# Differential attention: a wait per head for the rotated query, and one copy per unit for the turned probabilities, ahead of the next exponentials

## The reference, cut to what matters

```python
q = (h @ wq).reshape(B, L, N_HEADS, 2, HEAD_DIM)
q = partial_rope(q, pos) * (HEAD_DIM ** -0.5)
...
s = jnp.einsum('bqhcd,bkhcd->bhcqk', qblk, k).astype(jnp.float32)
...
p = jax.nn.softmax(s, axis=-1)
a = p[:, :, 0] - lam * p[:, :, 1]
return jnp.einsum('bhqk,bkhe->bqhe', a.astype(v.dtype), v)
```

## Time and profile before

| | us |
|---|---|
| median of 3 runs | 3104.79 |
| the three runs | 3104.3, 3104.79, 3112.43 |
| the profiled execution | 3102.6 |
| its span, first to last instruction | 3100.6 |

### The profile page before, as it was taken

One profiled execution on the slowest core, in us unless ns is written; L12 is line 12 of the kernel. 1 busy time (PEld: TensorE's weight loads), 2 busy tenths in 40 slices (PEclk: granted clock), 3 DMA queues, 4 the chain that ended last, 5 costly groups with the idle time before them and its releaser, 6 DMA issues.

```text
span 3100.6 us, 61224 instructions
## 1 busy us (share of the span) xinstructions
PE 2918.1 (94%) x21508; PEld 2783.9 (90%) x21508; DVE 2027.0 (65%) x4439; ACT 1544.0 (50%) x3349; POOL 583.7 (19%) x632
## 2 busy tenths in 40 slices
PE   8898889999999988889989999999989999999998
PEld 7688879999999987788889999999878799986998
DVE  6759877677677655578877666666573655555565
ACT  7442345555555544542445555555543455554554
POOL 4512670010010033015720000000130310012100
PEclk9899999999999988799999999999985999998899
DMA  4045317676676533145146555555441045541454
GB/s 154 16 130 164 113 58 224 210 232 223 210 230 205 183 117 109 55 141 166 61 146 209 184 183 183 183 183 183 156 129 55 1 135 185 169 130 34 143 183 136
DMA packets 140810, 458.19 MB, mean 148 GB/s; under 512 B 15792, under 2 KB 33584, under 8 KB 140656
## 3 DMA queue, kind: packets, MB, share of 16 engines
q1 hardware_dynamic: 135120, 436.75, 44.7%
q0 software_dynamic: 5536, 19.47, 2.2%
HBM read 446.65 MB, written 9.50 MB: 147 GB/s over the span
## 4 chain that ended last, share of the span: by engine, by line
PE 87%; DVE 5%; ACT 4%; POOL 2%; issue 1%; DMA 0%; DVEq 0%; POOLq 0%; ACTq 0%; SPq 0%
PE banks L784 64%; PE banks L941 7%; PE banks L964 3%; PE banks L1063 2%; PE banks L805 2%; POOL x_lo L2393 2%; PE banks L861 1%; PE banks L1149 1%; ACT w_hi L501 1%; PE banks L1179 1%; ACT arena L1389 1%; PE banks L1227 1%; PE banks L815 1%; ACT arena L1673 1%; DVE onehot L1987 1%
## 5 line engine op out<-in xcount | busy, mean ns | idle before, releaser
L508 DVE TENSOR_TENSOR w_lo<-ring,w_hi 128x512 fp32r<-128x512 f32 x1464 | 1019.5, 703 | 748.0 <-ACT w_hi L501 741.1
L501 ACT ACTIVATE w_hi<-ring 128x512 fp32r<-128x512 f32 x1464 | 916.7, 631 | 928.1 <-PE banks L784 885.7
L784 PE MATMUL banks<-x_hi,w_hi 128*128 128x256 f32 (+2 forms) x3136 | 911.2, 291 | 46.5 <-POOL x_lo L2393 21.3
L784 PE MATMUL banks<-x_lo,w_hi 128*128 128x256 f32 (+2 forms) x3136 | 902.0, 288 | 0.0
L784 PE MATMUL banks<-x_hi,w_lo 128*128 128x256 f32 (+2 forms) x3136 | 899.6, 287 | 0.0
L784 PE MATMUL banks<-gated_hi,w_hi 128*128 128x256 f32 x2560 | 727.3, 284 | 10.0 <-DVE gated_lo L2046 9.8
L784 PE MATMUL banks<-gated_hi,w_lo 128*128 128x256 f32 x2560 | 726.7, 284 | 0.0
L784 PE MATMUL banks<-gated_lo,w_hi 128*128 128x256 f32 x2560 | 725.5, 283 | 0.0
L784 PEld LDWEIGHTS banks<-x_hi,w_hi 128*128 128x128 f32 x3136 | 609.4, 194 | 57.6 <-issue 39.8
L784 PEld LDWEIGHTS banks<-x_lo,w_hi 128*128 128x128 f32 x3136 | 609.8, 194 | 0.6
L784 PEld LDWEIGHTS banks<-x_hi,w_lo 128*128 128x128 f32 x3136 | 610.3, 195 | 0.0
(11 more groups left out here) (325 smaller groups left out, 2941.5 us busy)
## 6 DMA issues: line engine op xcount, KB each, us to landing
ring<-in_peer_v SPq DMA_DIRECT2D x256, 512.0 KB, 3.6
ring<-in_peer_u SPq DMA_DIRECT2D x192, 512.0 KB, 3.5
arena<-in_peer_u SPq DMA_DIRECT2D x64, 512.0 KB, 3.6
ring<-in_mlp_up SPq DMA_DIRECT2D x64, 512.0 KB, 3.5
ring<-in_mlp_down SPq DMA_DIRECT2D x64, 512.0 KB, 3.5
ring<-w_peer_query SPq DMA_DIRECT2D x32, 512.0 KB, 3.5
ring<-w_fox_proj SPq DMA_DIRECT2D x24, 512.0 KB, 3.5
ring<-w_nsa_proj SPq DMA_DIRECT2D x20, 512.0 KB, 3.5
```

Of the source, the lines that this page charges most:

```text
L501: act.activation(w_hi[:, hn % SPLITS], raw_half(hn), ACT.Copy).then_inc(hi_ready, 1)
L508: dve.tensor_tensor(w_lo[:, hn % SPLITS], raw_half(hn), w_hi[:, hn % SPLITS].bitcast(F32), ALU.subtract)\
L784: mm = pe.matmul(out, w_at(w), x, start=start and j == 0, stop=stop and j == 2, skip_group_check=True)
```

## The change

Three edits, all in `attend_diff` of TensorE and ACT. The one wait for all eight heads becomes a wait per unit of the first query block for its own head. The 16-row piece of the first block moves next to the full one (column 128), and one copy of 256 or 384 columns with all 128 partitions takes the place of two. And `store(u-2)` moves ahead of `exps(u)` in ACT's round, and so ahead of the table load in round 16.

```diff
                 def scores(u):
                     t, hd, nk, _ = diff_unit(u)
+                    if u < HEADS:
+                        pe.wait_ge(rope_lo, NC + hd + 1)
                     if u >= 2:
                         pe.wait_ge(exp_done, u - 1)
...
-                        at = kt * P if kn == P else 2 * P
+                        at = kt * P
...
                 pe.wait_ge(tri_rounded, 1)
-                pe.wait_ge(rope_lo, 2 * NC)
                 for u in range(n_units + 3):
...
                 def store(u):
-                    full = (u // HEADS + 1) * P
+                    full = len(diff_unit(u)[3]) * P
                     act.wait_ge(turned, u + 1)
                     if u >= 2:
                         act.wait_ge(av_done, u - 1)
-                    act.activation(probsT[:, u % 2, 0:full], banks[:, 4 + u % 2, 0:full], ACT.Copy)
-                    act.activation(probsT[0:META, u % 2, 2 * P:3 * P], banks[0:META, 4 + u % 2, 2 * P:3 * P], ACT.Copy)                       .then_inc(turned_stored, 1)
+                    act.activation(probsT[:, u % 2, 0:full], banks[:, 4 + u % 2, 0:full], ACT.Copy).then_inc(turned_stored, 1)
...
                 for u in range(n_units + 3):
+                    if 2 <= u < n_units + 2:
+                        store(u - 2)
                     if u < n_units:
                         exps(u)
                     if u == n_units:
                         load_root_table()
-                    if 2 <= u < n_units + 2:
-                        store(u - 2)
```

## The result

The changed kernel took 3115.94 us, the median of six runs (3112.8 to 3117.39), against 3104.55 us of the kernel before on the same chip (six runs, 3097.15 to 3112.43). The ratio is 1.0036, 95% interval 1.0025 to 1.0048: slower by 11.4 us, just over the 0.3% that can be told from no change. The forecast was 3103.6 us with a range of 3096 to 3110. The profiled execution took 3115.64 us, 3113.6 of them its span.

The account below looks back on a forecast made before the run. TensorE, at half clock in 11 of the 16 units, was taken to bound the attention stage. Gains of 0.7 + 0 + 0.5 = 1.2 us, taken from 3104.8, gave 3103.6 us, with a range of 3096 to 3110.

Parts of the forecast that it names:

- What bounds the kernel: Attention stage: TensorE sets the pace at half clock in 11 of 16 units, so ACT savings there go unseen.
- Part 1: Start of the stage: with a wait per head, scores start earlier, lambda is late next, and 0.73 us are kept.
- Part 2: Rounds of the stage: one copy for two saves ACT 2.4 us in 16 units, worth nothing beside saturated TensorE.
- Part 3: Round 16: the copy ahead of the table load ends weigh(15) at 1280.85 instead of 1281.37, a gain of 0.5 us.
- The sum: Whole kernel: 0.7 + 0 + 0.5 = 1.2 us faster, 3104.8 - 1.2 = 3103.6 us; forecast as worked out, 58%.
- From there TensorE is saturated as before, so 0.73 us are kept: From scores(2), near 1230.24 instead of 1230.97: TensorE works without a gap, so the 0.73 us gain lasts.
- My own list of signs: Profile after: earlier first scores, a 4 us TensorE gap before scores(2), copies of 0.38 and 0.48 us, later half-clock stretch.
- rival C: End of the stage: clock stays at 1.2 GHz, slower by +3.7 - 0.7 = +3.0 us, 3107.8; chance 15%.
- Rival B: Rounds 3 to 13: clock returns early or never falls, gaining 13.8 us, 3089.8; 8% over 8 us, 7% smaller.
- The rule weighed there: First rounds: by the skill's rule activity releases the clock soon; 43.5 us of busy TensorE at 0.50 spoke against it.
- None of the cases reaches 3114: Whole kernel: no case gets that slow; 3% left for a median that falls among slow executions.

Follow-up runs that it names:

- e11: Changed kernel plus 16 already-met waits in ACT's stream behind the root, which restore the stream's old length; 3104.55 us, ratio 1.0002.
- e12: Changed kernel with two copies per unit again, still ahead of the exponentials, and with the waits per head; 3105.43 us, ratio 1.0012.
- e4: Kernel before with one copy per unit, placed ahead of the exponentials, but still the one wait for all heads; 3104.64 us, ratio 1.0016.
- e1: Changed kernel run again, unchanged but for a comment; 3115.3 us, ratio 1.0038.
- e9: Changed kernel plus 23 unused matmuls behind the scores of unit 1 in the differential attention, none ahead of the forgetting attention; 3087.7 us, ratio 0.9953.
- e10: Kernel before plus 23 unused matmuls behind the scores of unit 1 in the differential attention; 3093.79 us, ratio 0.9974.
- e5: Kernel before plus one unused DVE instruction at the end of the forgetting attention's projection; 3113.52 us, ratio 1.0033.
- e6: Changed kernel plus three unused DVE instructions at the end of the forgetting attention's projection; 3107.93 us, ratio 1.0007.

## Why the prediction was wrong, point by point

- **What bounds the kernel** held: TensorE's clock, and not ACT, sets the stage. That it sets more than this stage was not asked.
- **Part 1, 0.73 us.** Right in mechanism, with lambda as what is late next; 0.62 us came, up to round 3.
- **Part 2, nothing.** The copies took 384 and 486 ns for 0.38 and 0.48, and in the stage they gave next to nothing (68.35 us in e11, 68.50 with two copies in e12). But "worth nothing there" took the cost of removed instructions for their time on the engine alone. 16 instructions fewer put 0.29 us of pause into the chain 1400 us later.
- **Part 3, 0.5 us.** Right in size: 0.38 us in the kernel after, 0.49 us for the stage in e4. Its make-up differs, so part of that is luck. The forecast said that TensorE would lose its 0.62 us of idle time; it lost it ahead of weigh(14) and has 0.67 us ahead of weigh(15) instead (0.56 in e1 and e4), where 0.1 had been worked out.
- **The sum, -1.2 us.** Its terms came; the stage still came out 1.53 us longer, and 0.3 us in the repeats. The step that failed inside the stage is "From there TensorE is saturated as before, so 0.73 us are kept". My own list of signs said that the stretch of clock 0.50 would begin later and last about as long. It did so: 44.4 us before (1226.58 to 1270.94), 44.4 in e1 and e11. But it begins 3.4 us later against the work, since TensorE is at work 2.0 us longer ahead of its wait, so it ends 3.4 us later (55.0 us behind the last query block in e11, 51.6 before), in round 15. The profiled execution had 47.8 us of it. That is rival C, which I gave 15%.
- **Rival C's size.** Its terms were 1.7 for round 14, 1.0 for round 15, 1.0 for the end; measured 1.71 (from 0.47 early to 1.24 late), 0.68 (from 1.24 to 1.92 late), and none, since the clock came back ahead of the end, which kept its 0.38 us.
- **Rival B.** It did not occur by itself. Its price was near, in part by luck: it was 15.0 us for the kernel (to 3089.8), and e9, which holds the clock by filling, took 3087.7, 14.0 us less than the kernel before on its chip (3101.67); in the stage the gain was larger, 68.03 to 50.37 us. The bound of 2.20 us a round was that of the second block; the first takes 1.86.
- **The rule weighed there.** What the rows of the forecast showed, 43.5 us of unbroken work at 0.50, was shown again in the forgetting attention, 46.00 of 46.00 us. The Trainium skill, TensorE: Matmul & The Clock Gate, Part 1, says that the throttled state is the default and that activity releases it; the trace agrees for the full-height matmuls of the fill in e10 (back in 6.8 us), and not for the mix of half-height scores, transposes and products of these stages, which was at work without a gap for 47.00 and 46.00 us at the lower level.
- **"None of the cases reaches 3114", 3% slower.** This is the step that failed as a whole, and the larger one: the sum has no term for what stands behind the stage. All cases counted the stage alone, and took everything behind it as unchanged because its instructions are. The forgetting attention alone came out 11.5 us longer (64.56 to 76.06), and with 16 waits given back to ACT it did not (e11). Neither of the signs of being wrong that the prediction named, the clock at the upper level in the first block or maxima that do not start behind lambda, looked there, and neither came. The trace of before had the sign: the clock falls in a wait of 4.78 us ahead of the forgetting attention, 0.07 us ahead of its first matmul, and a stage of 64.6 us hangs on where in that wait it falls.
- **The chances.** 8% below the range and some 10% above it leave 82% within, not the 90% that is given.

Open: how the instruction transfer on q14 and the pause of 0.33 us hang together. That the pause moves with the number of instructions is shown by e11, with waits that do no work, and by e12; that a transfer starts behind each is shown too; that ACT stands still because its stream is not there yet is the likely reading, and no view shows it. How the changed start of the differential attention reaches L805, 1400 us later, as 0.1 to 0.2 us was not followed. Why the clock comes back at 20.5 us or at 37.5 to 47.8 us is known by its condition only, not by its mechanism: between 0.57 and 0.79 us there is no profile, and 3.77 us has an early return again.

## What to carry to other kernels

Before an edit is costed at nothing outside its stage, read the granted clock of the whole span, list the stages that begin behind an idle TensorE with a fall of the clock, and price each as it stands on either side of that fall: here one was worth 11.5 us, ten times the gain that was forecast. A shift of the work against the clock's low stretch is a term of the sum and not a side case. And a gap of TensorE ahead of rounds that could run at full clock is worth a try at filling. Where the first rounds behind it hardly waited for another engine, 23 unused matmuls made the stage 18 us shorter; where they waited 1.36 us, 20 of them left theirs as long as it was (81.0 us from the first score, for 80.7). That this wait is the reason rests on these two cases.

## What the runs showed of the hardware that I had not expected

- With the same instructions and the same idle time before them, the clock was back at 2.4 GHz after 20.5 us in eight profiles and after 47.8 us in two; the fall was 0.57 us or less ahead of the first matmul in the eight, 0.79 and 0.92 in the two.
- 0.9 us of added delay cost about 9 us (e5), and some 2.9 us gained 7.4 (e6 against e1).
- TensorE at work for 46.00 of 46.00 us stays at 1.2 GHz in the forgetting attention, and for 47.00 of 47.00 in the differential one.
- 16 instructions of ACT that do no work, at 1280 us, move a pause of 0.33 us near 2700 us off the chain and take away 10.8 us (3115.3 in e1, 3104.55 in e11).
- Such pauses of 0.33 us go with a transfer on an instruction queue, q14, that starts 0.7 to 1.5 us behind the late instruction.
